# A sum of squares moved from GpSimd to TensorE, and a mask table folded into matmuls with a new order of work, in a four-layer decoder step

## The chip, the cores and the metric

The kernel runs on one core of a Trainium2 chip. The metric is the device time of one execution in microseconds (us). A core has five engines that run their own instruction queues in order and meet through semaphores: TensorE (PE in the profile; PEld is its weight load), VectorE (DVE), ScalarE (ACT), GpSimd (POOL) and SyncE (SP), which issues most of the DMAs.

## The reference

One inference step of a trunk of four layers: a state-space scan (SSD) mixer, a dilated sliding-window attention, a differential attention, and an SSD mixer again, each followed by a SwiGLU feed-forward. 256 prompt tokens and 8 x 4 sample tokens go through the same weights in fp32. Two pieces matter here. The SSD mixer ends in a gated norm over four groups of 512 channels:

```python
gated = (y.reshape(bt, L, D_INNER) * jax.nn.silu(z)).reshape(bt, L, SSM_GROUPS, D_INNER // SSM_GROUPS)
y = rmsnorm(gated, norm_g.reshape(SSM_GROUPS, D_INNER // SSM_GROUPS)).reshape(bt, L, D_INNER)
return y @ w_out, new_conv, new_state
```

The window attention of the sample tokens adds a bias by relative distance to the scores, and bars keys out of the window:

```python
s = jnp.einsum('bthd,btnhd->bthn', q, kg) * (HEAD_DIM ** -0.5)
s = s + bias_tab[rel_bucket(n * dil)].T
s = jnp.where(valid[:, None, :], s, -jnp.inf)
lse = jax.nn.logsumexp(s, axis=-1)
```

## The kernel before

Activations lie with channels on the 128 partitions and the 288 tokens along the free axis. Each layer is a mixer phase or several, then a chain of output projection and feed-forward. Between phases all engines meet. In a phase every engine has a list of instructions written out by hand; a wait holds all that stands behind it on its engine. Weights come in blocks of 1 MB through SyncE, are split by ScalarE (L229) and VectorE (L240) into a high and a low part, and are used by L268 and L276.

**The scan phase (`ssd`, layers 0 and 3).** It walks 16 chunks of 128 channels, step k = 0 to 15. In a step TensorE runs one weight block in small pieces, and between the pieces the work of chunk k - 1 and k: states, decays, outer products, `y_inside`, `y_across` (L1099). VectorE gates a chunk (L1695), ScalarE squares the gated chunk (L1404) into one of the four slots of `sq`, GpSimd adds squares 1, 2 and 3 of a group onto slot 0 (`add_square`, L1239), and TensorE sums the 128 channels with a matmul of ones (`sum_squares`, L1104). ScalarE makes the reciprocal root of the sum (`root`, L1411, L1415) and VectorE scales (L1704). The sums of groups 0, 1 and 2 stand at the ends of steps 6, 10 and 14. The last one stands behind the loop, behind `turn_tail` (L1114), which transposes the rows that ScalarE then moves (`move_tail`, L1424) before it squares chunks 14 and 15. fp32 matmuls show as two records each, and L268 and L276, which work in fp32r, as one.

**The window-attention phase (`swa`, layer 1).** It has two strands. The eight prompt units u (two query tiles by four heads per group) go through `unit_scores` (TensorE, L2240), `unit_lowest` (VectorE, L2401), `unit_exp` (ScalarE), `unit_scale` (VectorE), `unit_turn` (TensorE, L2252), `unit_move` (ScalarE, L2348), `unit_values` (TensorE, L2265) and `unit_out` (VectorE, L2417). Units 0 to 3 have one key tile, 4 to 7 two. The sample strand takes two rounds q of four samples: `turn(q, part, ...)` transposes cached keys (L2157), in pieces that ScalarE moves when even and VectorE when odd (L2327, L2323), then `scores_wide` (L2178), `scores_rest`, the least of the negated scores (L2468), the exponential, `turn_probs`, `values` (L2219), `stage_out` and `turn_out`. Transposed pieces use three PSUM banks in turn, in the order of the list `order`: piece n waits until piece n - 3 has been moved.

The bias of the sample scores is a table. `lay_tables` (VectorE, L2427) copies four rows of `rel_bias` into `LT`, `tables_` (TensorE, L2165) multiplies it with one-hot rows `oh`, `bar_keys` (VectorE, L2445, L2447) adds the mask `barred` (128 rows of 908 numbers, loaded as such) to the 896 old keys and to the 12 new ones, and `lay_new_keys` (L2457) spreads the 12 columns. The waits are separate: `lay_tables` waits for the four rows of `rel_bias`, `tables_` for the one-hot rows, `bar_keys` for the mask. `scores_wide(0)` waits for all of it, since it writes the banks that the tables use.

Of the kernel before, what the change touches and what calls it, by code (L numbers as in the profile page):

```python
# [23 lines left out]
ALU = mybir.AluOpType  # L24
ACT = mybir.ActivationFunctionType
# [131 lines left out]
def build_program(nc, A, O):  # L157
# [611 lines left out]
    def ssd(layer, nxt):  # L769
# [8 lines left out]
        with phase() as (block, sb):  # L778
# [40 lines left out]
             gated, squared, sq_added, sq_summed, y_logged, y_rstd, normed, tl_mm, tl_moved) = (  # L819
# [4 lines left out]
                     "z_ready", "gated", "gated_squared", "gated_squares_added", "squares_in", "y_logged", "y_rstd", "y_normed", "tail_turned",  # L824
# [130 lines left out]
            def _(pe):  # L955
# [146 lines left out]
                def sum_squares(g):  # L1102
                    pe.wait_ge(sq_added.sem, sq_added.at(3 * g + 3))
                    pe.matmul(ps[:, 6, 0:TOK], ones, sq[:, 0, :], start=True, stop=True,  # L1104
                              skip_group_check=True).then_inc(sq_summed.sem, sq_summed.inc())
# [38 lines left out]
                for k in range(1, CI):  # L1144
# [23 lines left out]
                    if k % 4 == 2 and k >= 6:  # L1168
                        g = k // 4 - 1
                        pe.wait_ge(e_ready.sem, e_ready.at(6 * k + 6))  # L1170
                        sum_squares(g)
# [10 lines left out]
                pe.wait_ge(ea_ready.sem, ea_ready.at(CI))  # L1182
                for q in range(2, 6):
                    turn_tail(q)
                sum_squares(GROUPS - 1)

            @block.gpsimd
            def _(pool):
# [46 lines left out]
                def add_square(c):  # L1235
                    pool.wait_ge(squared.sem, squared.at(c + 1))
                    if c % 4 > 1:
                        pool.wait_ge(sq_added.sem, sq_added.at(c // 4 * 3 + c % 4 - 1))
                    pool.tensor_tensor(sq[:, 0, :], sq[:, 0, :], sq[:, c % 4, :], ALU.add).then_inc(  # L1239
                        sq_added.sem, sq_added.inc())  # L1240

                for n in range(EARLY):
                    conv_ends(n)
                for k in range(CI):
# [6 lines left out]
                    if k % 2 == 0 and k >= 4:  # L1251
                        for c in (k - 4, k - 3):
                            if c % 4:
                                add_square(c)
# [5 lines left out]
                for c in range(CI - 3, CI):  # L1260
                    add_square(c)
# [739 lines left out]
    def swa(layer, nxt):  # L2001
# [38 lines left out]
        with phase() as (block, sb):  # L2040
# [7 lines left out]
            oh, barred = scratch[:, 0:N_OLD + 12], scratch[:, 1024:1024 + N_OLD + 12]  # L2048
# [14 lines left out]
            new_bias, rows_in, masks_in = S("new_bias"), S("bias_rows_loaded", 16), hankel_in  # L2063
# [11 lines left out]
            def turned_of(u):  # L2075
# [5 lines left out]
                     + keys_of(1, 1, 0, 8) + turned_of(6) + [("out", 0, 0), ("out", 0, 1)] + turned_of(7)  # L2081
# [60 lines left out]
            def _(pe):  # L2142
# [141 lines left out]
                unit_scores(4)  # L2284
# [7 lines left out]
                unit_turn(4)  # L2292
                turn(1, 0, 4, 8)
                unit_values(4)
# [843 lines left out]
```

## Time and profile before

| | |
|---|---|
| median of 3 runs (least, most) | 1989.6 us (1987.84 to 1992.38) |
| the profiled execution's own time | 1987.84 us |
| its span, first to last instruction | 1986.2 us |
| TensorE busy | 1855.8 us, 93% |
| VectorE, ScalarE, GpSimd busy | 60%, 49%, 26% |
| mean granted TensorE clock | 0.976 of full speed |

The busy share is an average over phases with different limits. Matmuls are pipelined and their ends are modelled, so starts of instructions on TensorE tell more than ends. The scan phase of layer 0 ends at 296.5 us, that of layer 3 at about 1713.5 us; the window-attention phase lies between 642.2 and 715 us. The granted clock is at full speed in most of the span, and at half at the starts of some phases.

### The profile page before, as it was taken

Reading aid. Unit: us, or ns where it says so; the run is one execution under the profiler, and the core shown is the slowest. Engines: PE = TensorE matmul, PEld = TensorE weight load, DVE = VectorE, ACT = ScalarE, POOL = GpSimd, SP = SyncE. Lnnn points to the kernel's source line nnn. Section 1 sums busy time; section 2 is a strip of 40 time slices with the busy share of each in tenths; the row PEclk is TensorE's granted clock in tenths of the full one; section 3 lists DMA queues with packets and bytes.
Section 4 is the critical chain, followed back from the end, with each engine's and each line's share of the span. In section 5 each row is a group of like instructions: output and inputs, shape, how many; then the busy total and the mean of one; then the engine's idle time right before and its main releaser. Section 6 shows DMA issues by size and latency. Waiting matters only on the chain. (4 is left out here: it accounts for less than half of the span.)

```text
span 1986.2 us, 37671 instructions
## 1 busy us (share of the span) xinstructions
PE 1855.8 (93%) x14666; PEld 1751.4 (88%) x14666; DVE 1183.3 (60%) x2053; ACT 972.6 (49%) x1630; POOL 516.9 (26%) x545
## 2 busy tenths in 40 slices
PE   6999969999989989999997879999999999799999
PEld 4899959999989689999985659999988998699998
DVE  4788874555444565554446766555476889555544
ACT  3677773444343334433434554443347778444432
POOL 3223322343100323331103202333122222124410
PEclk9999989999999999999999998999999999899999
DMA  6368756555574846645748715655563777555654
GB/s 173 122 215 259 251 173 169 166 159 147 169 210 137 248 123 170 169 138 172 218 133 293 288 49 160 170 165 142 166 202 122 244 239 232 146 162 160 169 149 130
DMA packets 501690, 353.10 MB, mean 178 GB/s; under 512 B 14741, under 2 KB 486215, under 8 KB 500739
## 3 DMA queue, kind: packets, MB, share of 16 engines
q1 hardware_dynamic: 493644, 304.97, 52.8%
q0 software_dynamic: 7440, 45.43, 6.2%
q8 instruction: 118, 1.93, 0.4%
q14 instruction: 58, 0.48, 0.1%
q10 hardware_dynamic: 430, 0.29, 0.1%
HBM read 327.03 MB, written 50.63 MB: 190 GB/s over the span
## 5 line engine op out<-in xcount | busy, mean ns | idle before, releaser
L268 PE MATMUL ps<-xh,whi 128*128 128x288 f32 x2368 | 653.7, 302 | 10.0 <-PEq L176 9.8
L240 DVE TENSOR_TENSOR wlo<-raw,whi 128x2048 fp32r<-128x2048 f32 (+3 forms) x241 | 502.0, 2083 | 247.0 <-ACT whi L229 246.8
L268 PE MATMUL ps<-xl,whi 128*128 128x288 f32 x2368 | 643.4, 298 | 0.0
L229 ACT ACTIVATE whi<-raw 128x2048 fp32r<-128x2048 f32 (+3 forms) x241 | 419.2, 1740 | 260.0 <-PE ps L276 213.1
L268 PEld LDWEIGHTS ps<-xh,whi 128*128 128x128 f32 x2368 | 451.3, 191 | 12.5 <-issue 10.5
L268 PEld LDWEIGHTS ps<-xl,whi 128*128 128x128 f32 x2368 | 452.0, 191 | 0.7
L276 PE MATMUL ps<-xh,wlo 128*128 128x288 f32 x2368 | 352.5, 299 | 0.0
L276 PEld LDWEIGHTS ps<-xh,wlo 128*128 128x128 f32 x2368 | 326.5, 189 | 1.2
L535 POOL TENSOR_TENSOR gh<-sg,ut 128x288 f32<-128x288 f32 x88 | 216.3, 2458 | 353.0 <-ACT sg L470 353.0
L268 PE MATMUL ps<-hh,whi 128*128 128x288 f32 x704 | 189.7, 296 | 0.0
L268 PE MATMUL ps<-hl,whi 128*128 128x288 f32 x704 | 189.6, 297 | 0.0
L472 ACT ACTIVATE hh<-gh 128x288 fp32r<-128x288 f32 x88 | 39.1, 445 | 226.0 <-POOL gh L535 226.0
L268 PE MATMUL ps<-oh,whi 128*128 128x288 f32 x400 | 113.9, 311 | 26.4 <-PEq L176 15.1
L268 PEld LDWEIGHTS ps<-hl,whi 128*128 128x128 f32 x704 | 132.6, 188 | 0.0
L268 PEld LDWEIGHTS ps<-hh,whi 128*128 128x128 f32 x704 | 132.4, 188 | 0.0
L330 ACT ACTIVATE xh<-x,vec 128x288 fp32r<-128x288 f32 x64 | 33.9, 536 | 198.7 <-DVE x L495 117.6
L1232 POOL TENSOR_TENSOR E<-E,cb 128x288 f32<-128x288 f32 x64 | 57.5, 900 | 224.1 <-ACT E L1397 212.9
L268 PE MATMUL ps<-ol,whi 128*128 128x288 f32 x400 | 113.0, 307 | 0.0
L268 PEld LDWEIGHTS ps<-oh,whi 128*128 128x128 f32 x400 | 80.1, 200 | 29.0 <-issue 28.0
L276 PE MATMUL ps<-hh,wlo 128*128 128x288 f32 x704 | 104.2, 296 | 0.0
L345 POOL TENSOR_TENSOR sqx<-x 128x288 f32<-128x288 f32 x56 | 39.7, 709 | 245.6 <-DVE x L518 150.9
L512 DVE TENSOR_TENSOR hl<-gh,hh 128x288 fp32r<-128x288 f32 x88 | 40.3, 458 | 103.4 <-ACT hh L472 103.4
(326 smaller groups left out, 2639.9 us busy)
## 6 DMA issues: line engine op xcount, KB each, us to landing
raw<-in_ffn_w_in SPq DMA_DIRECT2D x176, 512.0 KB, 5.0
raw<-in_ssm_w_in SPq DMA_DIRECT2D x80, 512.0 KB, 5.1
raw<-in_ffn_w_out SPq DMA_DIRECT2D x64, 384.0 KB, 4.1
raw<-in_ffn_w_out SPq DMA_DIRECT2D x64, 320.0 KB, 3.3
H<-in_state_ssm SPq DMA_DIRECT2D x32, 512.0 KB, 4.4
out_ssm_sample<-H SPq DMA_DIRECT2D x32, 512.0 KB, 7.1
raw<-in_ssm_w_out SPq DMA_DIRECT2D x32, 512.0 KB, 5.4
Kp_L<-in_cache_diff_k SPq DMA_DIRECT2D x64, 256.0 KB, 4.7
```

What stands on the lines that cost most here:

```text
L229: act.activation(wts["hi"][:, s, 0:width], raw[:, s, 0:width], ACT.Copy).then_inc(hi_ready.sem, 1)
L240: dve.tensor_tensor(wts["lo"][:, s, 0:width], raw[:, s, 0:width], wts["hi"][:, s, 0:width].bitcast(F32), ALU.subtract).then_inc(lo_ready.s ...
L268: pe.matmul(out, W[0][:, kk, j, :], x_[:, k, :], stop=False, start=(part == 0 and kk == 0 and x_ is seg.hi), skip_group_check=True)
L276: mm = pe.matmul(out, W[1][:, kk, j, :], seg.hi[:, k, :], start=False, stop=(part == parts - 1 and end), skip_group_check=True)
L330: act.activation(th[:, c, :], x[:, c, :], ACT.Identity, scale=vec[:, 0, gain + c:gain + c + 1]).then_inc(xh_ready.sem, 1)
L345: pool.tensor_tensor(sqx[:, c % 2, :], x[:, c, :], x[:, c, :], ALU.mult).then_inc(sq_done.sem, 1)
L472: act.activation(hh[:, i, :], gh[:, r, :], ACT.Copy).then_inc(hid_hi.sem, hid_hi.inc())
L512: dve.tensor_tensor(hl[:, i, :], gh[:, r, :], hh[:, i, :].bitcast(F32), ALU.subtract).then_inc(hid_lo.sem, hid_lo.inc())
L535: pool.tensor_tensor(gh[:, r, :], sg[:, r, :], ut[:, r, :], ALU.mult).then_inc(gated_ready.sem, gated_ready.inc())
L1232: pool.tensor_tensor(E[:, h % 4, :], E[:, h % 4, :], cb[:, h // 8, :], ALU.mult).then_inc(w_ready.sem, w_ready.inc())
```

## The change

Two parts that don't touch each other.

1. In the scan, `add_square` on GpSimd is gone. TensorE sums the four squares of a group itself, with four matmuls that accumulate in PSUM. In the last group two of them stand ahead of `turn_tail(2)` to `turn_tail(5)` and two behind. GpSimd's second `weigh` of a step no longer stands behind the adds.
2. In the window attention the mask is four rows (T = 4 partitions of 908 numbers) with 128 columns more that hold a row-to-query pattern. `tables_` multiplies it in: each of its six ranges gets a second, accumulating matmul. ScalarE copies the finished bias of the old keys, VectorE the 12 columns (inside `lay_new_keys`). `bar_keys` is gone. All loads count on one semaphore, and `lay_tables` and `tables_` both wait for all six. With it goes another order of work on TensorE, ScalarE and VectorE.

```diff
-                def sum_squares(g):
-                    pe.wait_ge(sq_added.sem, sq_added.at(3 * g + 3))
-                    pe.matmul(ps[:, 6, 0:TOK], ones, sq[:, 0, :], start=True, stop=True,
-                              skip_group_check=True).then_inc(sq_summed.sem, sq_summed.inc())
+                def sum_squares(g, chunks):
+                    for c in chunks:
+                        pe.wait_ge(squared.sem, squared.at(c + 1))
+                        mm = pe.matmul(ps[:, 6, 0:TOK], ones, sq[:, c % 4, :], start=(c == 4 * g),
+                                       stop=(c == 4 * g + 3), skip_group_check=True)
+                    if c == 4 * g + 3:
+                        mm.then_inc(sq_summed.sem, sq_summed.inc())
...
+                sum_squares(GROUPS - 1, (CI - 4, CI - 3))
                 for q in range(2, 6):
                     turn_tail(q)
-                sum_squares(GROUPS - 1)
+                sum_squares(GROUPS - 1, (CI - 2, CI - 1))
...
-                    if k % 2 == 0 and k >= 4:
-                        for c in (k - 4, k - 3):
-                            if c % 4:
-                                add_square(c)
...
-                for c in range(CI - 3, CI):
-                    add_square(c)
...
+                     + keys_of(1, 1, 0, 8) + [("out", 0, 0), ("out", 0, 1)] + turned_of(6) + turned_of(7)
...
-                    sp.dma_start(rb[32 * t:32 * t + 32, :], A["rel_bias"]).then_inc(rows_in.sem, rows_in.inc())
+                    sp.dma_start(rb[32 * t:32 * t + 32, :], A["rel_bias"]).then_inc(loaded.sem, loaded.inc())
+                sp.dma_start(barred, A["barred_swa"]).then_inc(loaded.sem, loaded.inc())
                 sp.dma_start(oh, A["onehot_swa"]).then_inc(loaded.sem, loaded.inc())
-                sp.dma_start(barred, A["barred_swa"]).then_inc(masks_in.sem, masks_in.inc())
...
-                    pe.wait_ge(loaded.sem, loaded.at(1))
+                    pe.wait_ge(loaded.sem, loaded.at(T + 2))
...
-                        mm = pe.matmul(out, LT[:, g, :], oh[:, lo:lo + n], start=True, stop=True)
+                        pe.matmul(out, LT[:, g, :], oh[:, lo:lo + n], start=True, stop=False)
+                        mm = pe.matmul(out, barred[:, N_OLD + 12:], barred[:, lo:lo + n], start=False, stop=True)
...
                 unit_scores(1)
-                turn(0, 0, 3, 8)
+                turn(0, 0, 3, 6)
                 tables_()
                 unit_scores(2)
+                turn(0, 0, 6, 8)
                 unit_turn(0)
                 scores_wide(0)
                 unit_values(0)
+                unit_scores(3)
                 turn(0, 1, 0, 3)
                 unit_turn(1)
-                unit_scores(3)
                 unit_values(1)
+                unit_scores(4)
                 turn(0, 1, 3, 6)
                 unit_turn(2)
-                unit_scores(4)
                 unit_values(2)
...
                 unit_turn(4)
+                unit_values(4)
                 turn(1, 0, 4, 8)
-                unit_values(4)
...
                 unit_turn(5)
+                unit_values(5)
                 unit_scores(7)
-                unit_values(5)
...
+                turn_out(0)
                 unit_turn(6)
-                turn_out(0)
                 unit_values(6)
...
+                unit_exp(1)
+                act.wait_ge(tables.sem, tables.at(1))
+                act.activation(bias[:, 0:N_OLD], flat[:, 2560:2560 + N_OLD], ACT.Copy).then_inc(mixed.sem, mixed.inc())
                 keys(0, 0, 6, 8)
-                unit_exp(1)
...
-                    dve.wait_ge(rows_in.sem, rows_in.at(T))
+                    dve.wait_ge(loaded.sem, loaded.at(T + 2))
...
+                    dve.tensor_copy(base[:, :], ps[:, 7, 0:12]).then_inc(laid.sem, laid.inc())
...
                 keys(0, 0, 0, 3)
+                lay_queries()
                 lay_tables()
-                lay_queries()
                 unit_lowest(1)
-                keys(0, 0, 3, 8)
                 unit_scale(0)
-                bar_keys()
+                keys(0, 0, 3, 6)
                 unit_lowest(2)
+                lay_new_keys()
+                keys(0, 0, 6, 8)
                 unit_scale(1)
-                lay_new_keys()
+                unit_lowest(3)
                 unit_out(0)
                 keys(0, 1, 0, 3)
                 unit_scale(2)
-                unit_lowest(3)
+                unit_lowest(4)
                 unit_out(1)
                 keys(0, 1, 3, 6)
-                unit_lowest(4)
```

## Rows read from the trace of the kernel before

**Rows 1.** The page, part 1: busy time of each engine, whole span.

```profile
...
PE 1855.8 (93%) x14666; PEld 1751.4 (88%) x14666; DVE 1183.3 (60%) x2053; ACT 972.6 (49%) x1630; POOL 516.9 (26%) x545
...
```

**Rows 2.** TensorE's waits, 119.3 to 262.4 us: total, times, longest.

```profile
...
PE ps L1104 <- POOL sq L1239: 2.7, 3, 0.9
```

**Rows 3.** Timeline, 203 to 216 us: start, duration, instruction, idle before it.

```profile
...
214.66 0.30 PEld L1104 LDWEIGHTS ps<-sq,cst 128*128 128x128 f32 x2 [1.03 <-issue]
...
214.69 0.72 PE L1104 MATMUL ps<-sq,cst 128*128 128x288 f32 x2 [0.87 <-POOL sq L1239]
...
```

**Rows 4.** Timeline of TensorE, 1178.5 to 1185 us.

```profile
...
1178.70 6.09 PE L1786 MATMUL ps<-hsq,cst 128*128 128x288 f32 x24 [1.76 <-ACT hsq L1771]
```

**Rows 5.** Line L1695 (gate): ns least/median/most.

```profile
...
L1695 DVE TENSOR_TENSOR G<-yt,Zs x32: 437/440/1023, 127.5 to 1702.4; 128x288 f32<-128x288 f32 x32
...
```

**Rows 6.** Timeline, tail of the first scan phase.

```profile
...
280.88 1.91 PE L1114 MATMUL ps<-cst,tail 128*27 128x128 f32 x16
...
286.41 0.44 ACT L1404 ACTIVATE sq<-G 128x288 f32<-128x288 f32 x1 [1.22 <-DVE G L1695]
286.93 0.83 POOL L1239 TENSOR_TENSOR sq<-sq 128x288 f32<-128x288 f32 x1 [0.87 <-ACT sq L1404]
...
287.82 1.33 PE L1104 MATMUL ps<-sq,cst 128*128 128x288 f32 x2 [5.03 <-POOL sq L1239]
...
```

**Rows 7.** Stretches: busy us by engine, then PEclk, DMA share, GB/s.

```profile
...
286.00:287.00 1.00, 0.00 (x0) 0.00 (x0) 1.00 (x3) 0.44 (x1) 0.13 (x2) 0.95 0.25 74
288.00:289.00 1.00, 1.00 (x2) 0.31 (x2) 0.45 (x2) 0.00 (x0) 0.00 (x0) 0.50 0.00 0
300.00:302.00 2.00, 2.00 (x15) 2.00 (x15) 0.00 (x0) 0.00 (x0) 0.00 (x0) 0.86 1.11 308
649.00:650.00 1.00, 0.56 (x5) 0.59 (x6) 0.89 (x2) 0.00 (x0) 1.00 (x3) 1.00 1.01 398
...
```

**Rows 8.** Timeline, start of the window-attention phase.

```profile
...
645.61 0.43 SPq L2097 DMA_DIRECT2D scratch<-in_barred_swa  x1
...
646.30 1.03 DVE L2427 COPY LT<-rb 32x48 f32<-32x48 f32 x4 [1.35 <-DMA rb<-in_rel_bias]
...
649.44 1.06 PE L2157 MATMUL ps<-cst,K_L 128*128 128x128 f32 x8 [2.45 <-DVE KT L2323]
...
650.34 2.24 PE L2165 MATMUL ps<-scratch,LT 128*128 128x512 f32 x12
...
652.51 0.93 PE L2240 MATMUL ps<-QKV_L 64*128 64x128 f32 x6
...
654.24 1.92 PE L2178 MATMUL ps<-KT,Qall 128*32 128x512 f32 x16
...
654.57 1.46 DVE L2457 COPY BN<-base 32x12 f32<-32x12 f32 x8
...
```

**Rows 9.** DMA issues, 636 to 660 us: KB each, us to landing.

```profile
...
scratch<-in_barred_swa SPq DMA_DIRECT2D x1, 454.0 KB, 5.3
...
rb<-in_rel_bias SPq DMA_DIRECT2D x4, 1.5 KB, 2.2
```

**Rows 10.** Groups by line and shape, 642 to 715 us: busy, mean ns.

```profile
...
L2240 PE MATMUL ps<-QKV_L 64*128 64x256 f32 x24 | 6.2, 393 | 0.0
...
L2323 DVE COPY KT<-ps 128x512 f32<-128x512 f32 x8 | 5.4, 690 | 4.4 <-PE ps L2157 4.4
...
L2401 DVE CUSTOM_DVE_ANT_1 Su<-ps,BT_L 128x768 f32<-128x768 f32 x4 | 3.8, 958 | 3.0 <-PE ps L2240 2.9
...
L2165 PE MATMUL ps<-scratch,LT 128*128 128x256 f32 x2 | 0.6, 380 | 0.0
...
```

**Rows 11.** Timeline, unit 7 and the units before it.

```profile
...
698.33 1.19 DVE L2468 CUSTOM_DVE_ANT_0 scratch<-ps,bias 128x992 f32<-128x992 f32 x1 [2.11 <-PE ps L2194]
...
701.87 1.60 PE L2252 MATMUL ps<-DR,Su 128*128 128x128 f32 x12
...
704.11 1.49 PE L2265 MATMUL ps<-PTu,KV_L 128*64 128x128 f32 x12 [0.63 <-ACT PTu L2348]
...
```

More of the change, by code:

```diff
@@ L818, in ssd @@
              fs_mm, fs_moved, outer, updated, ys_mm, y_mm, yoff_mm, off_scaled, y_taken, off_added, z_scaled, z_ready,
-             gated, squared, sq_added, sq_summed, y_logged, y_rstd, normed, tl_mm, tl_moved) = (
+             gated, squared, sq_summed, y_logged, y_rstd, normed, tl_mm, tl_moved) = (
                  S(n) for n in (
@@ L823, in ssd @@
                      "y_state_product", "y_product", "y_off_product", "off_scaled", "y_taken", "off_added", "z_scaled",
-                     "z_ready", "gated", "gated_squared", "gated_squares_added", "squares_in", "y_logged", "y_rstd", "y_normed", "tail_turned",
+                     "z_ready", "gated", "gated_squared", "squares_in", "y_logged", "y_rstd", "y_normed", "tail_turned",
                      "tail_moved"))
@@ L1170, in _ @@
                         pe.wait_ge(e_ready.sem, e_ready.at(6 * k + 6))
-                        sum_squares(g)
+                        sum_squares(g, range(4 * g, 4 * g + 4))
                     if k == CI - 1:
@@ L1233, in weigh @@
                         w_ready.sem, w_ready.inc())
[L1235 to L1240, printed above, removed]
                 for n in range(EARLY):
@@ L2047, in swa @@
             Sb, PT = scratch[:, 0:1024], scratch[:, 1024:2048].rearrange("p (k n) -> p k n", n=P)
-            oh, barred = scratch[:, 0:N_OLD + 12], scratch[:, 1024:1024 + N_OLD + 12]
+            oh, barred = scratch[:, 0:N_OLD + 12], scratch[0:T, 1024:1024 + N_OLD + 12 + P]
             rb, LT = sb("rb", [P, NH]), sb("LT", [P, 3, P])
@@ L2062, in swa @@
             filled, laid, tables, mixed = S("buffers_filled"), S("tables_laid"), S("bias_tables"), S("bias_moved")
-            new_bias, rows_in, masks_in = S("new_bias"), S("bias_rows_loaded", 16), hankel_in
+            new_bias = S("new_bias")
             staged, half_out = S("out_staged"), o_moved
@@ L2080, in swa @@
                      + turned_of(4) + keys_of(1, 0, 4, 8) + [("prob", 0, 0), ("prob", 0, 1)] + turned_of(5)
-                     + keys_of(1, 1, 0, 8) + turned_of(6) + [("out", 0, 0), ("out", 0, 1)] + turned_of(7)
+                     + keys_of(1, 1, 0, 8) + [("out", 0, 0), ("out", 0, 1)] + turned_of(6) + turned_of(7)
                      + [("prob", 1, 0), ("prob", 1, 1), ("out", 1, 0), ("out", 1, 1)])
@@ L2440, in lay_queries, with lay_new_keys @@
                                 laid.sem, laid.inc())
-                def bar_keys():
+                def lay_new_keys():
                     dve.wait_ge(tables.sem, tables.at(1))
-                    dve.wait_ge(masks_in.sem, masks_in.at(1))
-                    dve.tensor_tensor(bias[:, 0:N_OLD], flat[:, 2560:2560 + N_OLD], barred[:, 0:N_OLD], ALU.add).then_inc(
-                        mixed.sem, mixed.inc())
-                    dve.tensor_tensor(base[:, :], ps[:, 7, 0:12], barred[:, N_OLD:], ALU.add).then_inc(
-                        laid.sem, laid.inc())
-                def lay_new_keys():
+                    dve.tensor_copy(base[:, :], ps[:, 7, 0:12]).then_inc(laid.sem, laid.inc())
                     dve.wait_ge(laid.sem, laid.at(9))
@@ L2516, in _ @@
                 unit_lowest(5)
-                keys(1, 0, 0, 8)
+                keys(1, 0, 0, 4)
                 unit_out(4)
+                keys(1, 0, 4, 8)
                 move(dve, copy, "prob", 0, 1)
@@ L3097, in shape_constants @@
     held = np.ascontiguousarray(parts[0:32].transpose(1, 0, 2).reshape(T * 32, -1))
-    barred = np.tile(parts[32] * np.float32(NEG), (P // T, 1)).astype(np.float32)
+    barred = np.concatenate([parts[32] * np.float32(NEG), i[None] % T == t], axis=1).astype(np.float32)
     dd = PAST + t - np.arange(PAST + T)[None]
```

## The prediction

> **What bounds the kernel now.** I read the page first: TensorE is busy for 93% of the span [rows 1], so a microsecond taken from its queue counts nearly anywhere, and I asked of each touched stretch what TensorE waits for there. The change touches two places: the scan phase, which runs twice (layers 0 and 3), and the window-attention phase, which runs once.
>
> In the scan loop the list of TensorE's waits, taken over the twelve steps from 119.3 to 262.4 us, has one entry: the wait for GpSimd's running sum of squares, three times for 0.9 us [rows 2]. The second scan layer gives the same. So the loop is bound by TensorE's own instructions, and the removed wait is all the slack there is. The timeline shows one such place: ScalarE has squared, GpSimd still adds, TensorE's weight port sits idle for 1.03 us, then the sum runs for 0.72 [rows 3]. Behind the loop the picture turns: the last group is a chain of gate, square, add, sum and root in which TensorE waits 5.03 us [rows 6], and nothing else ends the phase.
>
> In the window-attention phase no engine is full all the time, but TensorE walks a hand-written order, and from 649.4 us on it seldom stops. What the reader is to see in the timeline of its start [rows 8] is a 2.45 us wait for a key move of VectorE, behind it the tables of bias (2.17 us until the next instruction), and then scores, turn and the wide scores at 654.24.
>
> **The change part by part: the scan, middle groups.** Removed for each of groups 0 to 2: GpSimd's three adds and the idle 1.03 us. Added: three fp32 matmuls of 288 columns. Twenty-four records of the same form, two to a matmul, take 6.09 us [rows 4]; less the last one's latency of about 0.4 that is 0.247 a record, so 3 x 2 x 0.247 = 1.48 us. All squares but the last have long been ready and the last ends before TensorE gets there, so nothing is waited for; nothing hides the 1.48 either, by [rows 2]. Net +0.45 a group; six groups: +2.7 us. Bounds: +2.1 (if a second matmul on resident weights saves 0.1) to +3.3 (0.1 us of start-up each). The root that follows on ScalarE is behind a weight split and starts no later.
>
> **The last group.** Two of its matmuls are put ahead of the tail turns, two behind. The first two cost 0.99 us before the tail, which delays ScalarE's tail moves, four out_hi and square 14 by 0.99: square 14 would end at 286.18 instead of 285.19. ScalarE was idle 1.22 us before square 15, waiting for the gate of chunk 15 [rows 6], so it takes this: square 15 can run 286.15 to 286.60 instead of 286.41 to 286.85, provided the gate is ready. It is: the gate took 1.02 us while a GpSimd add ran beside it, and the median gate takes 0.44 [rows 5]. That is -0.25. The add of 0.83 and the two handovers around it (square end 286.85 to matmul start 287.82, less 0.1 that stays) give -0.87. And the sum itself took 1.33 us because the granted clock had fallen to 0.50 after four idle microseconds (from 282.8, where the tail turns end, to within 286 to 287) [rows 6, 7]; now TensorE is idle from 283.8 to 286.3 only, and an idle 2.45 us left the clock at 1.00 elsewhere [rows 7, 8], so it should take 0.72 as in the middle groups [rows 3]: -0.6. Sum -1.7 a layer, with bounds -0.55 (clock low, and both late matmuls in it) and -1.8. Two layers: -3.4. The Trainium skill (GPSIMD Engine Reference, Specifications) says that GpSimd shares its SBUF interfaces with VectorE and that instructions with two SBUF inputs contend; the 1.02 against 0.44 us agrees. Scan in all: 2.7 - 3.4 = -0.7 us.
>
> **Window attention, the start.** Before, laying the tables waited for the four small rows alone and ran at 646.30 [rows 8]. Now it waits for six transfers on one count, the 454 KB of one-hot rows among them. What the mask of 454 KB took, second in the pair, is 5.3 us to landing from an issue at 645.6 [rows 8, 9], so 650.9. The one-hot rows now have that place with 0.44 MB less ahead of them; at the 0.4 MB a microsecond that this stretch moved (398 GB/s [rows 7]) that is 1.2 us earlier: 649.7. Bounds: 650.9, and 647.8 (the 2.2 us of the small rows [rows 9]). Queued behind the waiting instruction on VectorE are the maximum of unit 1, the scale of unit 0 and key moves 3 and 5; on TensorE the tables, behind which stand the scores of unit 2 and everything else. Step by step from 649.7: four table copies 1.03, handover 0.1, tables start 650.85. They now have twice the matmuls, with the same columns, and matmuls of 64 rows here take no less than those of 128 rows (393 against 380 ns at 256 columns [rows 10]), so 2 x 2.17 = 4.34: 655.2. Scores of unit 2 to 656.1; on VectorE its maximum 0.6, the base copy 0.2, eight copies of new keys 1.46 (now ahead of key move 7, before behind it), key move 7 0.69 [rows 8, 10]: 659.1. The wide scores, which need that move, start there instead of at 654.24. TensorE's own queue (turn 6 and 7, 0.9, unit turn 0.87) would be ready at 657.8, so VectorE sets it. ScalarE's new bias copy, as long as the 1.1 us add that it replaces, ends at 656.3 and is hidden; if it weren't, it would have 2.8 us to lose. Net **+4.9 us** (+3.0 to +6.1 by the landing).
>
> **Window attention, the order behind it.** Before, between a unit's turn and its values stood other work (scores, a key turn), which covered ScalarE's move of the turned tile. Where nothing stands between them the trace has it once: unit 7's turn starts at 701.87, its values at 704.11, 0.63 us of idleness [rows 11]. The change makes this so for units 1, 2, 4, 5 and 6.
> Unit 1: +0.6.
> Unit 2: its four-tile scores now precede key turns 11 to 13. VectorE takes that maximum first (0.96 and its read, 1.04 [rows 10]), then the copy out 0.55, then key move 11 (0.55), on whose bank the turn of unit 2 waits: 3.75 us after the scores start, where TensorE is there after 2.66. That stall of 1.1 and the 0.65 of the move, less 0.3 of gaps that were there: +1.45.
> Unit 4: the values wait for ScalarE, which is in its 1.1 us exponential, but so did key turn 7 before (0.7 idle): -0.2.
> Unit 5: +0.7.
> Unit 6: the outputs are turned first; the second half of the unit's turn then waits for VectorE's copy of them, which is behind the 1.19 us minimum [rows 11]: 0.45, and the move after it 0.65, with small gaps gone: +1.0.
> Sum +3.55, bounds 0 (if the moved scores give back what the moves cost) and +4.5.
>
> **The sum.** -0.7 + 4.9 + 3.55 = +7.7 us. The profiled execution took 1987.84 us for a span of 1986.2; it was the fastest of three, whose median is 1989.6. I add to the median: 1997.3 us.
>
> **The rivals.**
> A. The clock falls in the attention phase. TensorE now has nothing from 647.0 to 650.85, 3.85 us; in the scan's tail the clock fell about 4 us behind the last matmul, and it came back within 300 to 302 us, about 3.8 us after the next phase began to multiply at 296.7 [rows 6, 7]; that long at half speed loses 1.9 us. Against it: 2.45 us did nothing here, and the gap is at the edge. It gives +9.6: 1999.2. The Trainium skill (TensorE: Matmul & The Clock Gate, HAM oscillation) warns that a wait between bursts puts the clock back to its lower level; by it this is the case to expect. The tail's 0.50 agrees.
> B. Smaller loss: the one-hot rows land near 648 and the early scores of units 3 and 4 shorten the exponential chain as much as the moves cost. For it: VectorE and ScalarE have idle time everywhere here. Against it: TensorE, not they, was the one without gaps. Start +3.2, order +1, scan -0.7: +3.5, 1993.1.
> C. Not slower: the scan loop isn't bound by TensorE's queue after all (the profile's ends are modelled), so that the 1.48 us a group are absorbed and the removed 1.03 comes through whole. Then the scan gives -6.2 - 3.4 = -9.6 against +8.45: -1.2, 1988.4. It decides where less than 0.13 of the added matmul time arrives (8.45 - 3.4 - 6.2 + 8.9a = 0). Against it stands [rows 2]: no other wait in 143 us.
>
> **How the numbers follow.** Forecast 0.42 (its own range 1995.5 to 1998.5), A 0.20, B 0.25, C 0.13. A measurement here tells 0.2%, 4 us, from no change. C ends a little faster or about level, half each; B straddles 4 us, and I give half of it to "same": faster 0.07, same 0.18, slower 0.75. The range leaves out most of C and A's far end (a landing at 650.9 and the low clock, +11.5): 1991.0 to 2000.5.
>
> **What would show it.** In the scan: no wait of TensorE at the sum of squares in the loop, the interval of four steps 47.7 + 0.45 us; in the tail the sum ending near 287.4 + 1.3 from the loop, with a granted clock near 1.00. In the attention phase: table copies at about 649.7, twelve more table matmuls, the wide scores some 5 us later, the phase's end some 8.5 later; new waits of values for ScalarE's moves. Wrong would be: the table copies within 2 us of 646.3, or a shorter stretch from the wide scores to the end.

## The result, and the profile after

The kernel after took 2002.55 us (median of 6 runs, 1997.28 to 2003.47), the kernel before 1988.72 beside it (6 runs, 1986.44 to 1992.38). The ratio is 1.0068, 95% interval [1.0052, 1.0085]: 13.8 us slower. Forecast were 7.7 us more and a range up to 2000.5 us. The direction was right, the size was not. After's profiled execution took 2008.17 us for a span of 2006.2, 5.6 us above the median, so below I set stretches of the two profiles against each other, not their spans.

The page of the kernel after, part 1 (it answers to [rows 1]): TensorE has 24 us more, which is more than its added matmuls cost.

```profile
...
PE 1880.2 (94%) x14726; PEld 1767.9 (88%) x14726; DVE 1172.7 (58%) x2052; ACT 974.2 (49%) x1631; POOL 498.9 (25%) x521
...
```

**The scan.** In the loop the only wait of [rows 2] has gone. The list of TensorE's waits in the kernel after, 119.3 to 262.4 us, is empty below its head, and the timeline shows the four matmuls (eight records) of group 2 following at once on the work before them.

```profile
core 0 of [0], span 2006.2 us
engine line waited for: us in total, times, longest us
```

```profile
...
262.24 0.39 PE L1099 MATMUL ps<-BC,S 128*128 128x128 f32 x2
262.46 2.11 PE L1105 MATMUL ps<-sq,cst 128*128 128x288 f32 x8
```

The tail, timeline of the kernel after (it answers to [rows 6]):

```profile
...
281.54 1.14 PE L1105 MATMUL ps<-sq,cst 128*128 128x288 f32 x4
...
282.51 1.91 PE L1117 MATMUL ps<-cst,tail 128*27 128x128 f32 x16
...
286.02 0.46 DVE L1686 TENSOR_TENSOR G<-yt,Zs 128x288 f32<-128x288 f32 x1
...
286.41 0.76 ACT L1395 ACTIVATE sq<-G 128x288 f32<-128x288 f32 x2
...
286.89 2.29 PE L1105 MATMUL ps<-sq,cst 128*128 128x288 f32 x4 [2.46 <-ACT sq L1395]
289.20 1.28 ACT L376 ACT_TABLE_LOAD   x1 [2.04 <-PE ps L1105]
```

The gate takes 0.46 us now that no GpSimd add runs beside it, and ScalarE squares chunks 14 and 15 back to back: both as forecast. But the last two matmuls take 2.29 us, for the granted clock had fallen again, as the rows of the stretches show (PEclk is the number behind the five engines):

```profile
...
284.00:286.00 2.00, 0.42 (x4) 0.15 (x2) 1.88 (x6) 2.00 (x6) 0.00 (x0) 1.00 0.90 230
286.00:287.00 1.00, 0.11 (x1) 0.12 (x1) 0.98 (x3) 1.00 (x4) 0.00 (x0) 0.79 0.38 119
...
```

The table load behind the sum starts at 289.20, 7.98 us behind the start of the last piece before the tail (L1099, 281.22); before it was 289.17 and 280.55, 8.62. The tail gave 0.64 us, not 1.7.

**Window attention, the start.** Timeline of the kernel after (it answers to [rows 8]):

```profile
...
640.97 2.02 SPq L2086 DMA_DIRECT2D rb<-in_rel_bias  x4
...
643.40 0.36 SPq L2088 DMA_DIRECT2D scratch<-in_onehot_swa  x1
...
647.23 1.02 DVE L2422 COPY LT<-rb 32x48 f32<-32x48 f32 x4 [2.86 <-DMA scratch<-in_onehot_swa]
...
648.31 2.03 PE L2156 MATMUL ps<-scratch,LT 128*128 128x512 f32 x2 [2.61 <-DVE LT L2422]
...
650.27 2.07 PE L2157 MATMUL ps<-scratch 4*128 4x512 f32 x2
...
659.12 1.64 PE L2232 MATMUL ps<-QKV_L 64*128 64x128 f32 x6
659.22 0.92 ACT L2355 ACTIVATE bias<-ps 128x896 f32<-128x896 f32 x1 [9.63 <-PE ps L2157]
...
660.80 0.56 DVE L2396 CUSTOM_DVE_ANT_1 Su<-ps,BT_L 128x384 f32<-128x384 f32 x1 [10.35 <-PE ps L2232]
...
663.87 1.83 PE L2170 MATMUL ps<-KT,Qall 128*32 128x512 f32 x8
...
```

VectorE waits 2.86 us for the one-hot rows, as the change says. What the reader is to see is the table matmuls: a pair of 512 columns takes 2.03 and 2.07 us, and the twelve reach from 648.31 to 659.12. That is 10.8 us where 4.34 were forecast. The stretches say why:

```profile
...
646.00:648.00 2.00, 0.00 (x0) 0.00 (x0) 0.69 (x3) 0.00 (x0) 2.00 (x5) 1.00 0.95 306
648.00:650.00 2.00, 1.69 (x2) 0.45 (x2) 1.92 (x7) 0.71 (x2) 2.00 (x4) 0.60 1.06 356
...
654.00:658.00 4.00, 4.00 (x12) 2.65 (x11) 0.00 (x0) 0.00 (x0) 4.00 (x8) 0.50 1.08 337
658.00:664.00 6.00, 6.00 (x29) 5.50 (x33) 2.85 (x14) 1.54 (x3) 3.08 (x7) 0.50 1.10 316
...
666.00:670.00 4.00, 3.98 (x35) 3.00 (x27) 1.71 (x6) 0.98 (x2) 0.00 (x0) 1.00 0.77 271
...
```

**The order behind it.** Waits of TensorE in the kernel after, from its timeline (L2257 are a unit's values, L2244 a unit's turn):

```profile
...
670.85 0.87 PE L2257 MATMUL ps<-PTu,KV_L 128*64 128x128 f32 x6 [0.58 <-ACT PTu L2341]
...
675.54 0.91 PE L2244 MATMUL ps<-DR,Su 128*128 128x128 f32 x6 [1.20 <-DVE KT L2316]
677.09 0.87 PE L2257 MATMUL ps<-PTu,KV_L 128*64 128x128 f32 x6 [0.64 <-ACT PTu L2341]
...
687.82 1.50 PE L2257 MATMUL ps<-PTu,KV_L 128*64 128x128 f32 x12 [0.63 <-ACT PTu L2341]
...
700.38 1.49 PE L2257 MATMUL ps<-PTu,KV_L 128*64 128x128 f32 x12 [0.63 <-ACT PTu L2341]
...
```

These are the forecast waits for ScalarE's move behind units 1, 2, 4 and 5, and the one of 1.20 us of unit 2's turn for a key move. From the wide scores to the phase's last cast (L483) it takes 65.02 us, before 60.81. The whole phase, first DMA to that cast, takes 87.92 us against 72.80: +15.1. The other phases are untouched; what they differ in between two executions is said below. Of the 20.0 us that the span of after's profile is longer, 15.1 lie in this phase, 6.1 in the untouched stretch between it and the scan of layer 3, and -0.2 in the loops and tails of the two scans; about -1 is spread over the rest.

### The profile page after: what moved, and what is told of

Read it like the earlier page. It is cut to its first block and busy times, and to the rows that moved or that the text cites. A ratio compares the mean times of both kernels' runs of the same rounds, so it can differ in the third digit from the quotient of the medians.

```text
span 2006.2 us, 37750 instructions
## 1 busy us (share of the span) xinstructions
PE 1880.2 (94%) x14726; PEld 1767.9 (88%) x14726; DVE 1172.7 (58%) x2052; ACT 974.2 (49%) x1631; POOL 498.9 (25%) x521
## 5 line engine op out<-in xcount | busy, mean ns | idle before, releaser
L268 PE MATMUL ps<-oh,whi 128*128 128x288 f32 x400 | 113.3, 309 | 26.4 <-PEq L176 15.1
```

What stands on the lines that cost most here:

```text
L268: pe.matmul(out, W[0][:, kk, j, :], x_[:, k, :], stop=False, start=(part == 0 and kk == 0 and x_ is seg.hi), skip_group_check=True)
```

## The experiments

For each kernel I give the ratio to the kernel before on the same chip; differences in us are worked out from this ratio unless they are said to be of medians. From its profiled execution I give the length of the window-attention phase, from its first DMA (L2095 before) to the cast L483, and that of the low clock in it. That length was 72.80 us before with no low clock, and 87.92 with 17.1 us of low clock after.

### The two parts alone

Kernel scan_only takes the diff's first part, swa_only its second.

> Before, with the scan part of the change alone. The two profiles say: each of six middle groups +0.42 us, each of two tails -0.64 us, so +1.2 us in all (1989.9), and the window attention as before. A rival: the scan part carries a good part of the 13.8 us, through the low clock in its tail or in the phase behind it; then +4 us or more.

> Before, with the window-attention part alone. The first theory (nearly all of the loss is here) expects +12 us, 2001; the phase 15 us longer in a profile where the clock falls at the tables. The rival (half of it in the scan) expects +7.

Measured: scan_only 1989.41 us, 1.0012 [1.0001, 1.0024]; swa_only 2002.65 us, 1.0073 [1.0058, 1.0088]. So the loss is the attention's, 14.5 us, as the first theory had it; the scan adds 2.4 (0.2 to 4.8). In swa_only's profile the phase takes 88.34 us, with 13.7 us of low clock from the tables on and 3.4 more at 677.5 us: the first part isn't needed for the low clock. The scan's 2.4 lies between the 1.2 expected and the rival's 4, and its interval excludes neither; its account by pieces is in the section on why the prediction was wrong.

### The order alone, and the order put back

Kernel order_only is the kernel before with the order of work of after:

```diff
                 unit_values(0)
+                unit_scores(3)
                 turn(0, 1, 0, 3)
                 unit_turn(1)
-                unit_scores(3)
                 unit_values(1)
+                unit_scores(4)
...
```

> Before, with the order of units 1 to 7 of after alone (scores 3 and 4 earlier, values right behind their turn, outputs ahead of turn 6); loads, tables and mask as before. The prediction's third term says +3.55 us, the profiles of before and after agree within 0.5: 1991.5, with waits of the values for ScalarE's moves. The rival (earlier scores give it back): within 1 us of before.

Measured 1993.34 us, 1.0025 [1.0014, 1.0036]: +5.0 us (2.8 to 7.2), by the medians 6.1. The rival, within 1 us of before, is out. Its phase takes 76.63 us, 3.8 more than before, with no low clock. From its timeline, the waits of 0.6 us for ScalarE's move and the one of 1.20 are there, and one more behind the turned outputs:

```profile
...
665.02 0.91 PE L2252 MATMUL ps<-DR,Su 128*128 128x128 f32 x6 [1.20 <-DVE KT L2323]
...
702.47 0.94 PE L2252 MATMUL ps<-DR,Su 128*128 128x128 f32 x6 [0.17 <-DVE OT_L L2489]
704.03 1.50 PE L2265 MATMUL ps<-PTu,KV_L 128*64 128x128 f32 x12 [0.63 <-ACT PTu L2348]
...
```

So the order costs 3.8 us in the phase by itself. Kernel old_order is the reverse, after with before's order:

> The kernel after with the order of work behind the tables put back to that of before (scores of units 3 and 4 later, something between each unit's turn and its values, the unit turn 6 ahead of the turned outputs). Theory: the order costs 5 us as it did alone, so about 1997.5 us, 1.0045 of before; the tables with their low clock are as in the kernel after. Rival (the low clock hides part of the order's cost, or the order hides part of the low clock's): 2000 us or more, or 1994 or less.

Measured 2001.58 us, 1.0065 [1.0048, 1.0083], above the theory's 1997.5 and on the rival's side (2000 or more), though its interval, 1997.5 to 2004.5 us, reaches down to the theory. Its profile has a landing later than any other (TensorE idle for 4.48 us ahead of the tables, 17.1 us of low clock) and a phase of 85.35 us. From the wide scores to the end it needs 60.55 us, before's 60.81, where every kernel with the new order needs 64.3 to 65.7. The order's cost is there in the trace; in the time of this one comparison it can't be seen, and the late landing, about 1.9 us, accounts for only a part of that.

### Is it the idle gap ahead of the tables?

The theory with which I began was rival A's: TensorE is idle for 2.6 us, so the clock falls. Kernel split_wait takes most of the gap away, kernel warm fills it with three fp32 matmuls of 512 columns.

```diff
-                    sp.dma_start(rb[32 * t:32 * t + 32, :], A["rel_bias"]).then_inc(loaded.sem, loaded.inc())
+                    sp.dma_start(rb[32 * t:32 * t + 32, :], A["rel_bias"]).then_inc(rows_in.sem, rows_in.inc())
...
-                    dve.wait_ge(loaded.sem, loaded.at(T + 2))
+                    dve.wait_ge(rows_in.sem, rows_in.at(T))
```

```diff
                 def tables_():
+                    for _ in range(3):
+                        pe.matmul(ps[:, 6, :], ident, KV[:, 0, 0, 0:512], start=True, stop=True)
                     pe.wait_ge(laid.sem, laid.at(8))
```

> After, but laying the tables waits for the four small rows alone, as before, and the tables for mask and one-hot rows; order and matmuls as in after. Theory 1 (TensorE's idle gap of 2.6 us at the tables drops the granted clock, and the low clock over tables and what follows costs some 7 us): the gap shrinks to 1 to 1.5 us, the clock stays at 1.00, and the kernel gains 7 to 9 us against after (1995). Theory 2 (the twelve extra matmuls themselves cost it, by their weight loads, whatever the clock): it gains only the 1 to 2 us of the wait (2001).

> After, with three fp32 matmuls of 512 columns (2.6 us, result unused) in TensorE's queue ahead of the wait for the tables. The wait stays as it is. Theory 1: the clock stays at 1.00, tables take some 4.5 us instead of 10.8, and the kernel gains about 6 to 7 us against after (1996). Theory 2: no gain, or a loss of up to 0.5 us (2003).

Measured: split_wait 2001.97 us, 1.0066 [1.0048, 1.0084]; warm 2001.13 us, 1.0058 [1.0041, 1.0076]. Neither gives back what the clock costs. The times are nearer to theory 2 (2001 and 2003) than to theory 1, but not for its reason: further down the same count of table matmuls takes 4.4 us at the full clock, weight loads included. The timeline of split_wait shows where it fell:

```profile
...
646.01 1.10 PE L2156 MATMUL ps<-scratch,LT 128*128 128x512 f32 x2 [1.26 <-DMA scratch<-in_onehot_swa]
647.04 1.15 PE L2157 MATMUL ps<-scratch 4*128 4x512 f32 x2
648.12 0.80 PE L2156 MATMUL ps<-scratch,LT 128*128 128x128 f32 x2
...
```

```profile
...
646.00:648.00 2.00, 1.99 (x4) 0.57 (x4) 0.67 (x2) 0.00 (x0) 2.00 (x5) 1.00 0.78 207
648.00:650.00 2.00, 2.00 (x6) 1.44 (x6) 0.00 (x0) 0.00 (x0) 2.00 (x4) 0.50 1.00 276
...
```

The first pair runs at full speed behind a gap of 1.26 us (1.10 and 1.15 us for 512 columns), then the clock falls while TensorE issues one table matmul after the other, and is low for 13.7 us. In warm TensorE is busy from 646.3 to 649.0 us and waits 1.82 more, and its clock too falls about 2 us into the tables (they start at 650.85) and is low for 13.7 us. The theory that the gap alone does it falls; a gap of 1.26 or 1.82 us was left in both.

### Is it the four-row matmuls?

The mask matmuls contract over 4 of the 128 rows. Kernel no_mask leaves them out, so that its scores get no mask. Kernel rows128 puts a second run of the 128-row table matmul in their place, so that the bias is doubled and no mask is added.

```diff
                         pe.matmul(out, LT[:, g, :], oh[:, lo:lo + n], start=True, stop=False)
-                        mm = pe.matmul(out, barred[:, N_OLD + 12:], barred[:, lo:lo + n], start=False, stop=True)
+                        mm = pe.matmul(out, LT[:, g, :], oh[:, lo:lo + n], start=False, stop=True)
```

> After, without the six mask matmuls: the mask is left out of the scores, the rest is as in after. Theory 3 (it is the matmuls of four rows in which the clock falls and stays low, not the idle gap ahead of them): the clock stays at 1.00 in spite of the gap of 2.6 us, the tables take 2.2 us, and the kernel comes to 1994 to 1996. Theory 1 in a weaker form (gap and light work together): the clock falls as in after, and the kernel comes to 1999 to 2001.

> After, with each mask matmul replaced by a second run of the 128-row matmul of its range: the same count, columns and weight loads, but 128 rows in place of four; the bias comes out doubled and without the mask. Theory 3: the clock stays at 1.00, the tables take 4.3 us, 1997. Theory 4 (count, order and tiny columns of the twelve matmuls make TensorE look little busy, whatever their rows): the clock falls as in after, 2002.

Measured: no_mask 1998.11 us, 1.0051 [1.0036, 1.0067], phase 80.95 us, low clock for 10.2; rows128 1999.69 us, 1.0063 [1.0045, 1.0082], phase 81.96 us, low clock for 3.4. Theory 3's clock of 1.00 came in neither, and both times lie between its figures and those of its rivals. Both keep the gap (2.28 and 2.87 us), and in both the clock fell within 0.5 us of its end. What differs is how it goes on. Timelines of no_mask and of rows128:

```profile
...
647.50 3.97 PE L2156 MATMUL ps<-scratch,LT 128*128 128x512 f32 x12 [2.28 <-DVE LT L2421]
...
```

```profile
...
648.49 2.08 PE L2156 MATMUL ps<-scratch,LT 128*128 128x512 f32 x2 [2.87 <-DVE LT L2422]
650.35 1.81 PE L2157 MATMUL ps<-scratch,LT 128*128 128x512 f32 x2
652.00 0.39 PE L2156 MATMUL ps<-scratch,LT 128*128 128x128 f32 x2
...
```

With as many matmuls and columns as after, all of them over 128 rows, the clock is back for the third matmul, and the twelve take 6.1 us instead of 10.8. So the four-row matmuls keep it low while the tables run, and the gap can start it.

Four rows are not all that keeps it low. In no_mask, with six 128-row matmuls and no four-row one, the clock was still low when the tables ended at 651.40 us, and stayed so for 6.8 us more, over scores of 64 rows, key turns, a unit's turn and most of the wide scores. In after it stayed low over the same work for 6.3 us behind the last four-row matmul. What that work does to the clock was not varied by itself.

### Neither gap nor four rows

This pointed to two causes, each of which leaves a low clock when the other is taken away. The next three kernels have split_wait's waits and, in turn, no mask matmuls, a second 128-row matmul, and after's own mask matmuls spread over 128 rows, of which 124 are zero (the same computation as after):

```diff
-            oh, barred = scratch[:, 0:N_OLD + 12], scratch[0:T, 1024:1024 + N_OLD + 12 + P]
+            oh, barred = scratch[:, 0:N_OLD + 12], scratch[:, 1024:1024 + N_OLD + 12 + P]
...
+                sp.wait_ge(filled.sem, filled.at(1))
+                sp.dma_start(barred[0:T, :], A["barred_swa"]).then_inc(loaded.sem, loaded.inc())
...
+                pool.memset(barred, 0.0).then_inc(filled.sem, filled.inc())
```

> The kernel after with two changes: the table copies wait for the four small rows alone (the table matmuls for the one-hot rows and the mask), and the six mask matmuls are left out (the scores get no mask). Theory (the gap of 2.3 to 2.9 us lowers the clock, and the four-row matmuls lower it or keep it low by themselves): with neither there is no low clock in the attention phase, the six table matmuls take 2.2 us, and the kernel takes about 1995 us, 6 above before (the order's 5 and the scan's 1.2). Rival (something else in the new start of the phase, such as the four key pieces turned before the tables instead of six, lets the clock fall): a low stretch of 3.4 us or more and 1997 us or more.

> The kernel after, the table copies waiting for the four small rows alone, and the six mask matmuls replaced by a second run of the 128-row table matmul (the bias doubled, no mask). As many matmuls and columns as after, and no gap ahead. Theory (rows occupied are what counts for the clock, and the gap): the clock stays at 1.00, the twelve matmuls take 4.3 us, the time is about 1997 us. Rival (the number of table matmuls, not their rows): low for 13 us as with four rows, about 2002 us.

> The kernel after, the table copies waiting for the four small rows alone, and the mask tile zeroed on all 128 partitions before its four rows are loaded into it, so that the six mask matmuls run over 128 rows of which 124 are zero; same result as after. If the clock goes by the rows that a matmul occupies, it stays at 1.00, the twelve matmuls take 4.3 us, and the time is about 1997 us. If it goes by what is multiplied (rows of zeros count as none), the clock is low for some 13 us as with four rows and the time is 2001 to 2002 us.

Timeline and stretch of padded_split (128x512 now over 128 rows):

```profile
...
645.17 1.10 PE L2158 MATMUL ps<-scratch,LT 128*128 128x512 f32 x2 [1.10 <-DMA scratch<-in_barred_swa]
646.11 1.02 PE L2159 MATMUL ps<-scratch 128*128 128x512 f32 x2
...
652.75 0.69 DVE L2318 COPY KT<-ps 128x512 f32<-128x512 f32 x1
...
653.55 1.92 PE L2172 MATMUL ps<-KT,Qall 128*32 128x512 f32 x16 [1.32 <-ACT PTu L2343]
...
```

```profile
...
646.00:648.00 2.00, 2.00 (x10) 1.36 (x9) 0.58 (x1) 0.00 (x0) 2.00 (x4) 1.00 0.88 291
648.00:650.00 2.00, 2.00 (x18) 1.93 (x17) 0.00 (x0) 0.29 (x1) 2.00 (x5) 1.00 0.88 266
...
```

The twelve matmuls take 4.4 us and the clock stays at 1.00 through the whole phase. The wide scores wait 1.32 us. The row names ScalarE's move, but that was over at 652.75; what ended just before them, at 653.44, is VectorE's key move, as the prediction had it. The seven kernels side by side:

| second matmul of a pair | gap ahead of the tables 2.3 to 2.9 us | gap 0.8 to 1.3 us |
|---|---|---|
| four rows | after: phase 87.92, low 17.1, ratio 1.0068 | split_wait: 84.92, low 13.7, 1.0066 |
| four rows padded to 128 | not run | padded_split: 78.50, low 0, 1.0041 [1.0026, 1.0055] |
| 128-row table matmul again | rows128: 81.96, low 3.4, 1.0063 | rows128_split: 78.21, low 0, 1.0045 [1.0028, 1.0061] |
| none | no_mask: 80.95, low 10.2, 1.0051 | no_mask_split: 77.73, low 3.4 (late, from 665.2 us), 1.0028 [1.0014, 1.0041] |

Taking away either cause shortens the phase by 3 to 7 us, taking away both by 9.4 to 10.2. All five profiles with four-row matmuls (after, swa_only, old_order, split_wait, warm) have 13.7 or 17.1 us of low clock from the tables on, the three with a short gap and without them none there. In the times a single cause taken away doesn't show (1.0051 to 1.0066 beside 1.0068, intervals about 0.0017 to either side). By the medians padded_split took 1996.31 (+8.3), rows128_split 1995.97 (+8.0) and no_mask_split 1992.98 (+5.0). By the ratios padded_split is 5.0 us faster than split_wait (0.4 to 9.6, the two half widths of 0.0018 and 0.0015 added in squares). What was changed between the two is the rows that the mask matmuls occupy, with the memset and the later load of 16 KB that this takes. The expectations for it and for rows128_split (1997 us, 4.3 us for the tables, the clock at 1.00) hold, and the rivals that count matmuls, or rows of zeros as none, are out. For no_mask_split the theory's 1995 us and 2.2 us for the tables hold in the main (1992.98 and 2.25); the late stretch of low clock is not explained.

### A version faster than both

In the scan's tail the removed wait for GpSimd gave something; in the loop three added matmuls cost more than the wait they replace, and one should cost less. Kernel hybrid is the kernel before; GpSimd adds only squares 1 and 2 of groups 0 to 2, TensorE sums slots 0 and 3, and in the last group it sums all four, each when it is there, behind all tail turns.

```diff
+                    slots = (0, 3) if g < GROUPS - 1 else (0, 1, 2, 3)
+                    for n in slots:
+                        if n != 0 or g == GROUPS - 1:
+                            pe.wait_ge(squared.sem, squared.at(4 * g + n + 1))
+                        mm = pe.matmul(ps[:, 6, 0:TOK], ones, sq[:, n, :], start=(n == 0), stop=(n == 3),
+                                       skip_group_check=True)
```

> Before, with another division of the sum of squares: in the three middle groups GpSimd adds squares 1 and 2 onto 0, and TensorE sums slots 0 and 3 with two matmuls; in the last group TensorE sums all four, behind the tail turns. By the rows of before: a middle group loses 1.03 us of waiting and gains one matmul of 0.49, -0.55 x 6; the tail loses the last add and nothing is put ahead of the turns, -1.0 to -1.5 each. Sum -5 to -6.5 us, 1982 to 1983. The rival: TensorE waits for the second add all the same, since both squares come at the end of the step; then -2 to -3.

Measured 1981.98 us (12 runs), 0.9975 [0.9963, 0.9988]: 5.3 us less than the kernel before beside it (2.4 to 7.4), and by the two ratios some 18 less than after. Timeline of its tail:

```profile
...
279.05 1.91 PE L1120 MATMUL ps<-cst,tail 128*27 128x128 f32 x16
...
280.80 1.14 PE L1109 MATMUL ps<-sq,cst 128*128 128x288 f32 x4
...
283.42 0.75 PE L1109 MATMUL ps<-sq,cst 128*128 128x288 f32 x2 [1.49 <-ACT sq L1408]
...
284.52 0.75 PE L1109 MATMUL ps<-sq,cst 128*128 128x288 f32 x2 [0.34 <-ACT sq L1408]
285.30 1.28 ACT L376 ACT_TABLE_LOAD   x1 [0.83 <-PE ps L1109]
...
```

```profile
...
284.00:286.00 2.00, 0.93 (x3) 0.30 (x2) 1.46 (x4) 1.15 (x2) 0.00 (x0) 1.00 0.18 54
286.00:287.00 1.00, 0.00 (x0) 0.00 (x0) 0.00 (x0) 0.99 (x2) 0.00 (x0) 0.92 0.00 0
...
```

The last idle times of TensorE are 1.49 and 0.34 us, the clock falls only between 286 and 287 us, behind the sum, and both late matmuls take 0.75 us each where after's two took 2.29 together. From the start of the first tail turn to the table load it needs 6.25 us; before it was 8.29. In the loop, from the first matmul of L1072 (there are two in each of the 16 steps) to the last, it takes 173.63 us, before 176.25, in layer 3 173.62 against 175.89.

Only 1.5 and 1.4 us of the loops' gains lie at the three sums (forecast 1.65 a layer). The rest, 1.1 and 0.9 us, lies in the last steps before the tail, where TensorE's clock was low for 3.4 us in hybrid and for 6.8 in the kernel before. That stretch is 3.4 us long in some tails of kernels with the scan part of the change and 6.8 in others, and 6.8 in all six of the kernels with GpSimd's adds as before; that hybrid's change is the cause is not shown. By loops and tails the profile has 9.0 us less than before, the times 5.3.

## Why the prediction was wrong, step by step

**What failed: the window attention's start, the term "2 x 2.17 = 4.34", and with it rival A's 1.9 us.** The doubling took the full clock for granted. The tables took 10.8 us, and all of TensorE's work from the tables to 665.4 us ran at half speed. At the full clock the step itself was right: from the first table matmul to the wide scores 8.25 us were forecast (650.85 to 659.1), padded_split takes 8.38 and rows128_split 8.37, and after takes 15.56. The landing went the other way: table copies 6.26 us after the phase's start, where 7.45 were forecast and 4.05 were before, so at full clock the term +4.9 would have been +3.7, and the low clock made +10.9 of it. That is a cost of 7.2 us, and 15.56 less 8.38 gives the same. Padded_split is the check on the whole phase: with the clock at 1.00 and the same number of matmuls the phase costs 5.7 us more than before, of which the order is 3.8.

Rival A named the low clock and gave it 0.20. Its mechanism (a gap of 3.85 us starts it, and it is back 3.8 us later) was at most half of it. The gap was 2.6 us, shorter than A asked for, and the length was taken from [rows 7], where full 128-row matmuls follow. Here four-row ones follow, and the low clock lasted 17.1 us. A's time of 1999.2 was 3.4 us short. The sentence "matmuls of 64 rows here take no less than those of 128 rows" was right in duration at a given clock and missed what rows do to the clock.

The prediction cited the Trainium skill (TensorE: Matmul & The Clock Gate, HAM oscillation), by which a wait between bursts puts the clock back. The kernels with the gap at the tables agree (low clock at once behind 2.87 us in rows128, which has no four-row matmul), but split_wait and warm don't: there the clock fell inside a burst of table matmuls. The same page (Part 1) says that the gate goes by how busy TensorE has been. The profile's busy time doesn't tell the cases apart: split_wait is busy for 3.99 of the 4.00 us from 646 to 650, where its clock falls, and padded_split for 4.00 of them with the clock at 1.00.

**The order: right.** Forecast +3.55, in order_only's profile +3.8, in its time +5.0 (2.8 to 7.2), and the waits that were named are in both traces: unit 1 0.58, unit 2 1.20 for the key move (forecast 1.1) and 0.64, units 4, 5 and 6 0.63 each; the second half of unit 6's turn waits 0.17 for the copy of the outputs, where 0.45 was forecast. It is the sum that was measured, not what each unit gained or lost. ScalarE's bias copy took 0.92 us beside TensorE's work and held nobody, as said.

**The scan's middle groups: right in kind, a third too dear.** At the first two sums the step from one L1072 to the next became 0.33 to 0.35 us longer (in layer 0 165.43 to 174.81 against 165.04 to 174.09), forecast 0.45; at the third 0.16 us in layer 0 and 0.28 in layer 3. The removed wait is gone and most of the added time is paid, so rival C, by which TensorE's added work is absorbed, is refuted. The interval of four steps that was to show it, from 212.76 to 260.40 us before, is 0.41 longer. The stretch behind the third sum, up to the last step's first L1072, became shorter (10.98 to 10.32 us in layer 0, 10.70 to 10.32 in layer 3), which I had not forecast and did not isolate. Over the whole loop that makes +0.3 us in layer 0 and +0.7 in layer 3, forecast +1.35 each.

**The tail: the term "-0.6" for the clock failed.** I let TensorE's two early matmuls keep the clock up because 2.45 idle us had not lowered it elsewhere. It was idle for 2.46 us, and the clock fell at the same place, between 286 and 287 us. What came is the lower bound that was named (-0.55): 0.64. But the clock does not always fall there. All ten kernels with the scan part have this same gap of 2.46 us in both tails. In 19 of the 20 the clock fell before the sum was done; in the first tail of rows128_split it stayed at 1.00, as the row shows, the sum took 1.24 us, and the tail gave 1.69 us, the forecast's 1.7:

```profile
...
285.84 1.24 PE L1105 MATMUL ps<-sq,cst 128*128 128x288 f32 x4 [2.46 <-ACT sq L1395]
...
```

So the rest of the tail's working was right, and the term was wrong because it took the rare case for the rule. Hybrid's tail, with matmuls at 280.80, 283.42 and 284.52, gives 2.04 us in both layers, with the full clock to the end of the sum. Whether the spread pieces held the clock, or the sum was just over before it fell (at 286.9 us, as in the kernel before), was not separated.

**What stays open.** By these stretches (loops and tails of the kernel after) the scan part is worth -0.2 us in all, near the -0.7 of the forecast; scan_only measured +2.4 (0.2 to 4.8). The rest would be in phases that the change doesn't touch, which differ by several us from one profiled execution to the next in the length of their own low-clock stretches: from the cast L483 to the first L1072 of layer 3 it takes 805.6 us before, 811.3 in scan_only, 808.0 in order_only and 803.7 in hybrid. The low clock in that stretch adds up to 47.8, 54.6, 47.8 and 41.0 us; in after it is 51.2 us of 811.7. Whether the scan part shifts them or chance does can't be read from one profile each. Open is also why idle gaps just before the tables (2.45 us in the kernel before, 2.58 in order_only, 2.33 in hybrid, all ahead of key turns) did not lower the clock, while 2.28 us did in no_mask; a gap's length alone does not decide it. The moment at which a gap falls, and the work on either side of it, were not varied with the length held.

## What to carry to other kernels

Before you fold a small addition into accumulating matmuls, look at the granted clock of the stretch and at the rows that the matmuls occupy: six of them over 4 rows made this phase 7.2 us longer (split_wait against no_mask_split), over 128 rows, zero-padded, 0.8 (padded_split). At a wait that ends a chain, let each piece of a last reduction run as soon as its input is there, as hybrid's sum of squares does, instead of adding on another engine first: it was worth 2.04 us a tail. That this also keeps the clock up is not shown. And read a clock from several executions or tails before a term rests on it: the same 2.46 us gap lowered it in 19 tails and not in one.

## What the runs showed of the hardware that I had not expected

The granted clock fell, and stayed at 0.50 for 13.7 to 17.1 us, while TensorE issued matmuls without a pause. In the tables, the first 9 to 11 us of the burst, every second one was over 4 rows; with the same columns over 128 rows, zeros in 124 of them, it stayed at 1.00 (padded_split), and after a gap it came back after 3.4 us (rows128). With six 128-row table matmuls and then scores of 64 rows, key turns and a unit's turn behind the gap it took 10.2 us (no_mask). At half clock 512 columns took 2.07 us over 4 rows and 2.03 over 128: the rows don't show in the duration, only in the clock. Each reading of the clock is from one profiled execution of each kernel. Among the kernels built on the whole change or its second part, the ratios, from 5 to 11 executions each, go the same way: 1.0028 to 1.0045 without a low clock at the tables, 1.0051 to 1.0073 with one. Within either group they don't tell the kernels apart.
